# A decoder trunk in split fp32: high and low moving parts in one 512-wide product, value chunks in pairs

## The reference

```
for i in range(2):
    proj = x @ w_in[i]                                   # 1024 x 17408
    attn = three dilated window attentions, 8 heads of 128, merged by their log-sum-exp
    ret  = chunkwise retention, 4 heads, keys 256, values 512, group norm, * silu(gate)
    m    = (sig(x Wg_a) * (attn @ w_attn_proj) + sig(x Wg_r) * (ret @ w_ret_proj)) @ w_out
    x    = LayerNorm(alpha * x + m)
    ple  = sigmoid(x @ w_ple_gate) * (p[i] @ w_ple_proj)
    h    = causal_conv3(x @ w_up) + conv_b               # 2 * 2816 columns, per feature
    x    = LayerNorm(alpha * x + (gelu(gate) * up) @ w_down + ple)
```

## Time and profile before

| | us |
|---|---|
| median of 3 runs | 1545.26 (1545.22 to 1547.12) |
| the profiled execution | 1545.38 |
| its span | 1543.6 |
| TensorE busy | 1525.7 (99%), 11746 products |
| VectorE busy | 919.1 (60%) |
| ScalarE busy | 743.5 (48%) |
| DMA | 265.60 MB, mean 172 GB/s |

### The profile page before, as it was taken

How to read it: one execution, slowest core, us unless ns; L and a number is a source line. 1 busy time by engine, 2 the same in 40 slices (tenths; PEclk the granted TensorE clock), 3 DMA queues, 4 the chain that set the end, 5 groups by cost and what they waited for, 6 DMA issues and landing times.

```text
span 1543.6 us, 27813 instructions
## 1 busy us (share of the span) xinstructions
PE 1525.7 (99%) x11746; PEld 1478.3 (96%) x11746; DVE 919.1 (60%) x1001; ACT 743.5 (48%) x783; POOL 22.9 (1%) x23
## 2 busy tenths in 40 slices
PE   8999999999999999999999999999999999999998
PEld 7999999999999989999999999999999999899997
DVE  5564653745644486666865636556465445776677
ACT  5444454444533345556544534545445333465553
POOL 0000000000000010000000000000000000100000
PEclk9999999999999999999999999999999999999999
DMA  8544544445446565656455544454454464655551
GB/s 287 185 146 155 177 151 163 136 163 163 164 152 205 177 207 176 205 176 218 164 164 164 164 153 163 136 176 148 150 181 145 165 218 151 218 191 188 179 196 63
DMA packets 231462, 265.60 MB, mean 172 GB/s; under 512 B 4192, under 2 KB 221792, under 8 KB 230880
## 3 DMA queue, kind: packets, MB, share of 16 engines
q1 hardware_dynamic: 231248, 264.44, 51.8%
q10 hardware_dynamic: 144, 0.13, 0.0%
HBM read 263.50 MB, written 1.05 MB: 171 GB/s over the span
## 4 chain that ended last, share of the span: by engine, by line
PE 93%; DVE 4%; DMA 1%; ACT 1%; issue 1%; SPq 0%; DVEq 0%
PE bank L1029 26%; PE bank L1030 26%; PE bank L1031 26%; PE acc L1029 3%; PE acc L1030 3%; PE acc L1031 3%; DVE w_lo L605 1%; PE acc L1126 1%; PE acc L1144 1%; PE acc L1111 1%; PE acc L1141 1%; PE acc L1128 1%; DVE stat L627 1%; DMA raw<-w_in 1%; ACT w_hi L360 0%
## 5 line engine op out<-in xcount | busy, mean ns | idle before, releaser
L605 DVE TENSOR_TENSOR w_lo<-raw,w_hi 128x2048 fp32r<-128x2048 f32 x241 | 551.6, 2291 | 449.7 <-ACT w_hi L360 449.4
L1029 PE MATMUL bank<-xT_hi,w_hi 128*128 128x256 f32 x2240 | 637.0, 284 | 0.1
L1031 PE MATMUL bank<-xT_hi,w_lo 128*128 128x256 f32 x2240 | 633.8, 283 | 0.0
L1030 PE MATMUL bank<-xT_lo,w_hi 128*128 128x256 f32 x2240 | 633.8, 283 | 0.0
L360 ACT ACTIVATE w_hi<-raw 128x2048 fp32r<-128x2048 f32 x243 | 463.8, 1910 | 158.0 <-PE bank L1031 98.6
L1029 PEld LDWEIGHTS bank<-xT_hi,w_hi 128*128 128x128 f32 x2240 | 429.8, 192 | 2.0 <-issue 0.5
L1030 PEld LDWEIGHTS bank<-xT_lo,w_hi 128*128 128x128 f32 x2240 | 429.8, 192 | 1.5
L1031 PEld LDWEIGHTS bank<-xT_hi,w_lo 128*128 128x128 f32 x2240 | 429.8, 192 | 0.0
L1029 PE MATMUL bank<-w_hi,xT_hi 128*128 128x256 f32 x768 | 219.7, 286 | 5.4 <-DVE w_lo L605 2.3
L1030 PE MATMUL bank<-w_lo,xT_hi 128*128 128x256 f32 x768 | 217.2, 283 | 0.0
L1031 PE MATMUL bank<-w_hi,xT_lo 128*128 128x256 f32 x768 | 217.2, 283 | 0.0
(11 more groups left out here) (155 smaller groups left out, 1445.2 us busy)
## 6 DMA issues: line engine op xcount, KB each, us to landing
raw<-w_in SPq DMA_DIRECT2D x135, 1024.0 KB, 5.0
raw<-w_up SPq DMA_DIRECT2D x44, 1024.0 KB, 5.1
raw<-w_down SPq DMA_DIRECT2D x20, 1024.0 KB, 5.2
raw<-w_ret_proj SPq DMA_DIRECT2D x16, 1024.0 KB, 5.2
raw<-w_attn_proj SPq DMA_DIRECT2D x8, 1024.0 KB, 5.1
raw<-w_out SPq DMA_DIRECT2D x8, 1024.0 KB, 5.1
raw<-w_ple_gate SPq DMA_DIRECT2D x8, 1024.0 KB, 5.1
scratch<-ln_rows SPq DMA_DIRECT2D x4, 1024.0 KB, 7.0
```

The source lines that it names most:

```text
L605: nc.vector.tensor_tensor(w_lo[:, s, :], raw[:, s, :], w_hi[:, s, :].bitcast(F32), ALU.subtract).then_inc(lo_ready, 1)
L1029: mm(dst, st_hi, mv_hi, start=start, stop=False)
L1030: mm(dst, st_hi, mv_lo, start=False, stop=False)
L1031: return mm(dst, st_lo, mv_hi, start=False, stop=stop)
```

## The change

- **Merge and MLP (`both_parts`).** High and low parts of the moving operands (`xT_both`, `attn`, `ret`) now lie side by side. The high weights are multiplied with both in one 512-wide product: columns 0 to 255 hold high x high, 256 to 511 high x low. The product low x high, 256 wide, is added to the right part. A chunk fills two banks (a `pair`). ScalarE copies the right part out, VectorE adds the left part from PSUM to it, and what follows (sigmoid, centre tap) reads the sum. The very last up chunk of a layer stays in three narrow products (`one_part`).
- **Value chunks in pairs (`two_chunks`).** Two neighbouring slots of the weight ring are the moving operand of one 512-wide product, for retention values and for values of groups 1 and 2; one token half fills one bank. Both chunks must be ready at the start, both are freed at the end. Since a pair must not wrap round the ring, the order of a mixer differs between the layers (`VALUES`). The first pair of layer 0 stays as it was.
- **Written out.** The loops over mixers and merges become Python loops on all engines; the MLP keeps its loop.
- **Orders.** In a mixer the second `scores` stands behind chunk 13, VectorE's second mask and the group statistics stand at chunk 14 ahead of `to_lo`. In the first merge attention stands behind the first retention chunk. In the MLP `to_hi` and `to_lo` of the next chunk stand between take and centre or taps.

The core of the diff:

```diff
+VALUES = ((0, 2, 12, (11, 14)), (1, 0, 11, (13, 14)))   # rv, v0, v12, g01 of each layer
...
+            def both_parts(l, g, c, p, src, k0=0, first=True, last=True):
+                weights_ready(g, c)
+                hi, lo = w_hi[:, slot(l, c), :], w_lo[:, slot(l, c), :]
+                for m in range(2):
+                    for k in range(KT):
+                        o = k * CH + m * P
+                        mm(pair[p][:, m, :], hi[:, o:o + P], src[:, k0 + k, :, :].rearrange("p a t -> p (a t)"),
+                           start=first and k == 0, stop=False)
+                        ins = mm(pair[p][:, m, SEQ:2 * SEQ], lo[:, o:o + P], src[:, k0 + k, 0, :],
+                                 start=False, stop=last and k == KT - 1)
+                ins.then_inc(chunk_done, 1)
...
+            def two_chunks(l, c, b, t, ks=range(KT)):
+                s = slot(l, c)
+                for k in ks:
+                    ins = split_product(bank[b][:, :].rearrange("p (u n) -> p u n", u=2),
+                                        xT_hi[:, k, t * P:(t + 1) * P], xT_lo[:, k, t * P:(t + 1) * P],
+                                        w_hi[:, s:s + 2, k * CH:(k + 1) * CH], w_lo[:, s:s + 2, k * CH:(k + 1) * CH],
+                                        k == 0, k == KT - 1)
+                if t:
+                    ins.then_inc(chunk_done, 2)
+                elif ks[-1] == KT - 1:
+                    ins.then_inc(tile_done, 1)
...
     # ScalarE, MLP
+                def take_low(g, c, half, n):
+                    act.wait_ge(chunk_done, g + c + 1 + RING)
+                    act.wait_ge(mid_ready, n)
+                    nc.scalar.activation(hpad[:, 2 * half:2 * half + 2, 2:2 + SEQ], pair[half][:, :, SEQ:2 * SEQ],
+                                         ACT.Copy).then_inc(up_low, 1)
+                def take_centre(half, i):
+                    act.wait_ge(bank_read[2 * half], value(i + (l * USES[2 * half] + U_MLP[2 * half] + 2)))
+                    centre(hpad[:, 2 * half:2 * half + 2, 2:2 + SEQ], half, i).then_inc(up_centre, 1)
...
                 def steady(g, r, i):
                     to_hi(l, g, r, 3)
                     to_hi(l, g, r, 4)
                     mid_high(n)
-                    take_h(g, 2, 0, n, i + 1)
+                    take_low(g, 2, 0, n)
                     to_hi(l, g, r, 5)
+                    take_centre(0, value(i + 1))
                     gelu(value(l * NF + i + 1))
-                    take_h(g, 3, 1, n, i + 1)
+                    take_low(g, 3, 1, n)
+                    take_centre(1, value(i + 1))
...
     # VectorE, MLP
+                def up_sum(half, i):
+                    dve.wait_ge(up_low, value(2 * i + (l * (2 * NF - 1) + half + 1)))
+                    v = hpad[:, 2 * half:2 * half + 2, 2:2 + SEQ]
+                    nc.vector.tensor_tensor(v, pair[half][:, :, 0:SEQ], v, ALU.add).then_inc(bank_read[2 * half], 1)
...
                 def steady(g, i):
                     to_lo(l, g, 3)
                     to_lo(l, g, 4)
-                    gated(turn, value(nm + i + 1))
-                    taps(0, next_turn, i + 1)
+                    gated(value(l * NF + i), value(nm + i + 1))
+                    up_sum(0, value(i + 1))
                     to_lo(l, g, 5)
-                    taps(1, next_turn, i + 1)
+                    taps(0, value(i + 1))
+                    up_sum(1, value(i + 1))
+                    taps(1, value(i + 1))
...
     # TensorE, first merge
-                gate(g, 1, 1, 0)
-                attend((l + 1) * NJ)
-                pe.wait_ge(ret_affine, (l + 1) * NJ + 1)
-                pe.wait_ge(ret_lo_ready, (l + 1) * NJ)
-                mixers(g, 2, 0)
+                gate(g + 1, 1, 0)
+                pe.wait_ge(ret_affine, (l + 1) * NJ + 1)
+                transpose_prob((l + 1) * 2 * NJ)
+                pe.wait_ge(ret_lo_ready, (l + 1) * NJ)
+                pair_free(0, U_MERGE[0] + 1)
+                both_parts(l, L0, g + 2, 0, ret, 0, last=False)
+                attend((l + 1) * NJ)
+                both_parts(l, L0, g + 3, 0, ret, KT, first=False)
```

More of the change, by code:

```diff
@@ L183, in program @@
         half_neg = stat[:, 60:62]
-        bank = [ctx.enter_context(nc.psum_tensor(f"bank{i}", [P, 512], F32)) for i in range(4)]
+        pair = [ctx.enter_context(nc.psum_tensor(f"bank{i}", [P, 2, 512], F32)) for i in range(2)]
+        bank = [pair[i // 2][:, i % 2, :] for i in range(4)]
         acc = [ctx.enter_context(nc.psum_tensor(f"acc{i}", [P, 512], F32)) for i in range(4)]
-        ret_yT = (bank[3], acc[3])
         raw_loaded = [sem(f"raw_loaded{s}") for s in range(RING)]
@@ L726, in mixer @@
             def mixer(l, j):
-                it = value(l * NJ + j)
-                it2 = value(it * 2)
-                g = value(l * C_LAYER + j * C_MIX)
-                first = isinstance(j, int)
+                it = l * NJ + j
+                it2 = it * 2
+                g = l * C_LAYER + j * C_MIX
+                rv, v0, v12, g01 = VALUES[l]
+                one_by_one = l == 0 and j == 0
                 def rotate(i):
@@ new lines, in group_stats @@
+                def group_stats():
+                    dve.wait_ge(ret_av_done, it + 1)
+                    for t, av in enumerate((bank[3], acc[3])):
+                        ins = nc.vector.bn_stats(st_gn[:, t * 6:(t + 1) * 6], av[:, :])
+                    ins.then_inc(gn_stats, 1)
+                    dve.wait_ge(gn_stats, it + 1)
+                    nc.vector.memset(stat[:, 75:76], 0.0)
+                    for t in range(TT):
+                        ins = nc.vector.bn_aggr(mv_gn[:, t, :], st_gn[:, t * 6:(t + 1) * 6])
+                    ins.then_inc(gn_mean_var, 1)
+                    dve.wait_ge(gn_mean_var, it + 1)
+                    nc.vector.tensor_scalar(ve_gn, mv_gn[:, :, 1], GN_EPS, None, ALU.add).then_inc(gn_var_eps, 1)
@@ L804, in mixer @@
+                    if not l and j and c == 1:
+                        finish_ret(j - 1, it)
                     if c == 9:
@@ L910, in taps @@
                             ins.then_inc(conv_first, 1)
[L911 removed]
+                            dve.wait_ge(conv_first, value(2 * turn + (half + 1)))
                     ins.then_inc(conv_ready, 1)
@@ L1010, in _ @@
                 group_rstd(l, 0)
-                with pool.Fori(1, NJ) as j:
+                for j in range(1, NJ):
                     group_rstd(l, j)
@@ L1132, in mixer, with bank_free @@
             def mixer(l, j):
-                it = value(l * NJ + j)
-                it2 = value(it * 2)
-                g = value(l * C_LAYER + j * C_MIX)
-                used = [value(l * USES[b] + j * 5) for b in range(3)]
-                first = isinstance(j, int)
+                it = l * NJ + j
+                it2 = it * 2
+                g = l * C_LAYER + j * C_MIX
+                used = [l * USES[b] + j * 5 for b in range(3)]
+                rv, v0, v12, g01 = VALUES[l]
+                def bank_free(c):
+                    pe.wait_ge(bank_read[c % 3], used[c % 3] + c // 3 + 1)
                 def scores(a):
@@ L1216, in mixer @@
                         ins.then_inc(ret_av_done, 1)
+                begin = 0 if j else 3
+                if not j and not l:
+                    bank_free(0)
+                    x_tile_ready(0, 0)
+                    pe.wait_ge(first_lo, 1)
+                    token_half(l, 0, 0, 0, range(4))
+                    pe.wait_ge(x_in[1], 16)
+                    for h in range(2):
+                        transpose_half(0, 1, h)
+                    weights_ready(g, 0)
+                    token_half(l, 0, 0, 0, range(4, KT))
+                    x_tile_ready(0, 1)
+                    token_half(l, 0, 0, 1)
+                    for c in (1, 2):
+                        bank_free(c)
+                        by_token(l, g, c, c)
+                if not j and l:
+                    x_tile_ready(2 * l, 0)
+                    bank_free(0)
+                    weights_ready(g, 0)
+                    token_half(l, 0, 0, 0)
+                    bank_free(1)
+                    weights_ready(g, 2)
+                    two_chunks(l, 1, 1, 0, range(4))
+                    transpose_x(2 * l - 1, 1)
+                    two_chunks(l, 1, 1, 0, range(4, KT))
+                    x_tile_ready(2 * l, 1)
+                    token_half(l, 0, 0, 1)
+                    bank_free(2)
+                    two_chunks(l, 1, 2, 1)
+                for c in range(begin, C_MIX):
+                    if c in (rv + 1, v12 + 1):
+                        behind(c)
+                        continue
+                    bank_free(c)
+                    if c in (rv, v12):
+                        weights_ready(g, c + 1)
+                        two_chunks(l, c, c % 3, 0)
+                        bank_free(c + 1)
+                        two_chunks(l, c, (c + 1) % 3, 1)
+                    elif c == v0:
+                        by_token(l, g, c, c % 3)
```

(4 more changed lines are left out.)

549 lines of the change are left out of this document (312 added, 237 removed).

## The result

| | before | after |
|---|---|---|
| median of the runs shown | 1545.24 us (1545.13 to 1547.12) | 1578.25 us (1576.58 to 1580.46) |
| profiled execution, its span | 1545.38, 1543.6 | 1578.85, 1577.0 |
| mean granted clock | 0.999 | 0.993 |

What follows compares the result with a forecast made beforehand. TensorE, 99% busy with matmuls, was taken to bound the kernel. Terms -8.4 - 9.6 + 27.8 + 5.0 + 5.3 + 0.2 + 3 = +23.3 us on 1545.4 gave 1569; range 1552 to 1582, own mechanism 1558 to 1576.

Steps and rivals of the forecast that it cites:

- The ring: MLP loop: ScalarE and VectorE's chain of waits sets a period of 17.25 us against 16.98; TensorE waits 0.7 per iteration.
- Rival 1: MLP: the ring doesn't bind and TensorE sets the pace throughout, 1529 us; chance 0.11, and 0.04 for a half-way case.
- The tail: Written-out MLP end: TensorE waits 4.6, 0.6, 2.6 and 5.0 us; the whole MLP stage +13.9 a layer.
- Products: Merge and MLP chunks: a wide and narrow pair takes 346.5 ns, 0.21 us saved per chunk, 8.4 us outside the MLP.
- the prediction's own sign: TensorE: the prediction is wrong if the MLP shows no waits or wide steps differ from 226.5 ns.
- Value pairs: Mixers: a pair of value chunks takes 48 x 226.5 ns, 0.64 us less; 15 pairs save 9.6 us.
- layer 1's mixers: Layer 1: pairs find their weights 3 us early; mixers about 1.3 us shorter each, -5.1 for the stage.
- Between gated mixture and MLP: From the gated mixture's start to the first MLP chunk: forecast 0 change.
- Mixers of layer 0: Value pairs wait 1.8 us for their second weight chunk, three times, +5.3 us; the stage +0.8.
- Merges' waits: New copies and sums cost +1.35 us at the last merge and +1.1 at the first, a layer; together +5.0.
- Clock: Behind the MLP's last long wait: six to twelve products at half clock, 1.5 us a layer, +3.
- rival 3: MLP tails: cold clock spreads, each of four long waits costs 3 us, bare; 1578 us, chance 0.12.

Runs made afterwards that it cites:

- e1: Changed kernel, in the MLP loop alone ScalarE forms the centre tap before copying the next weights and VectorE runs taps before splitting them; 1566.2 us, ratio 1.0136.
- e4: Changed kernel with the MLP's wide and narrow up chunks as 48 products of 256 columns again, takes, sums and order kept; 1578.14 us, ratio 1.0213.
- e3: Changed kernel with a tile's eight wide products first and its eight narrow ones after, instead of by turns; 1575.03 us, ratio 1.02.
- e7: Changed kernel with e2, e3 and e5 together, bank 3 awaited only before the second up half, last weights' copy and split one turn earlier; 1545.53 us.
- e5: Changed kernel, in layer 0's mixers VectorE splits the value pair's second weight chunk ahead of mask and group statistics; 1571.84 us, ratio 1.0166.
- e2: As e1, and in the written-out MLP tail too the centre and taps come before the next weights' copy and split; 1558.47 us, ratio 1.0083.
- e6: Changed kernel with useless wide products (17 and 18) filling TensorE's two long waits in each MLP tail; 1575.01 us, ratio 1.0187.
- e8: As e7, with the tail's next to last w_down chunk copied and split one place earlier; 1550.64 us, ratio 1.0029.
- e9: As e8, with VectorE's residual and last-weight split cut into halves between sums and taps, and ScalarE's last-weight copy ahead of its rounding; 1540.22 us, ratio 0.9962.
- e11: As e9, with ScalarE's take of the whole last up half ahead of GELU in each MLP tail; 1531.78 us, ratio 0.991.
- e10: As e9, with 15 useless wide products in TensorE's wait for each layer's last intermediate; 1536.74 us, ratio 0.9942.

## Why the prediction was right, and where it was off

- **The ring.** Right: 17.30 us measured for 17.25, take to taps 4.62 for 4.71. TensorE's wait in each turn is 0.3 in the rows where 0.7 was foretold, since its own turn is 16.8 and not 16.5. e1 takes the order away and the loss with it, e4 takes the products away and nothing happens. Rival 1 (the ring doesn't bind) is out.
- **The tail.** Right in kind and nearly in size: waits of 4.3 and 4.7 us for 4.6 and 5.0; the stage +14.65 for +13.9. The 2.6 us for weights foretold between them came as 0.64 (layer 0) and 1.59 (layer 1).
- **Products.** The mis-sized term. The prediction put a pair at 226.5 + 120 = 346.5 ns everywhere; by turns it takes 353.4 in the merges and nearly everywhere in the MLP, and only a few MLP chunks have 347. By the prediction's own sign (wide steps that differ from 226.5) this part failed: by turns a wide step is 230 to 240 ns. In the merges, of a layer's 4.2 us, 2.1 arrived: 4.3 us of the miss. In the MLP it was hidden in after; it makes TensorE's turn 16.79 instead of 16.5 in e1. e3 shows half of it to be the order of the two widths (350 in groups); why the other 3.5 ns stay, and why a few chunks are quicker, no run tells. Value pairs step at 227 ns as taken, and layer 1's mixers gave 4.7 of 5.1.
- **Between gated mixture and MLP.** Missed: the written-out entry waits for banks 1 and 3 ahead of the first half, and bank 3 is read last. 1.0 us a layer; e7 removed it. The step "a change adds a wait, who is queued behind it" wasn't made for this one.
- **Mixers of layer 0.** Three waits of 1.95, 1.63 and 1.63 us where 1.8 each were foretold, gone in e5. The stage is 1.7 over its forecast all the same. 0.8 of that is the kernel's start. In after TensorE's first products on weights step by 213 ns until 14.4 us, in before by 120 (after above, before below, the two rows three products apart):

```profile
12.00 0.41 PE L1179 MATMUL bank<-w_hi,xT_both 128*128 128x256 f32 x1
...
12.64 0.41 PE L1179 MATMUL bank<-w_hi,xT_both 128*128 128x256 f32 x1
```

```profile
11.73 0.28 PE L1029 MATMUL bank<-w_hi,xT_hi 128*128 128x256 f32 x1
...
12.09 0.28 PE L1029 MATMUL bank<-w_hi,xT_hi 128*128 128x256 f32 x1
```

  At one and the same product of the first mixer, some 62 us in, after is 0.8 us behind before, e4 0.75 ahead, e2 and e6 1.45 behind. From there to the first merge the stage is 1.7 us longer than before in after, e3, e4 and e6 alike, so 0.9 over the forecast. 0.6 of the 0.9 is the price of the waits: without them e5 passes this stretch 5.9 us faster, where 5.3 was put down. In e1 and e2 the stretch is 3.3 us longer than before: there the clock stood at its lower level for 3.4 us behind the first of the three waits. The 213 ns are 256 columns at 1.2 GHz, so the start was slow by the clock, it seems; the profile's record of the clock begins only at 14.4 us in after, and doesn't show it.
- **Merges' waits.** 1.35 on the last, as worked out; 0.9 us of 1.1 at the first retention chunk.
- **Clock.** +3 forecast; in e6 the last products were 4.3 us shorter in sum and the MLP 1.5 longer, and the median fell by 3.2. The Trainium skill (TensorE: Matmul & The Clock Gate, "Why this matters for your kernels") advises against idle gaps between bursts; the waits of 4.3 and 4.7 us, followed by 6.7 us at half clock each in layer 0 and by 3.4 in layer 1, agree.
- **A number shared with a rival.** The result is the very figure of rival 3 (1578), but not by its mechanism. That rival had each of the four long waits cost 3 us by the clock, 12 in all; e6 fills all four and gets 3.2 back. The difference to 1569 is made of the terms below.

Of the 33.5 us between the profiled executions the forecast had 23.3. The other 10.2: 4.3 from the pair's step, 2.0 from bank 3, 1.5 from the MLP, 2.1 from the mixers (0.8 of it the start), 0.3 behind it.

My later expectations were worse than the forecast. e2, e7 and e8 each took a wait's length for its price. In a tail of rings a wait that goes uncovers the next: from e7 on, where TensorE and the last intermediate came within 0.7 and 1.6 us of each other, only what brought both earlier (e9, e11) or kept the clock up (e10) made the kernel faster.

## What to carry to other kernels

A saving of 13 ns per folded product (in value pairs; 7 where widths go by turns) was real, but it was worth nothing until the order in which the two helper engines do their passes was redone: count the ring (who takes, who is queued between take and the next step) before the matmuls. Put long passes that nobody waits for into the places where the engine is idle within the chain, cut to the length of that idle time (here 2.2 us cut in two for slots of 1.16; the place and the cut were tried together only). Before moving a late split, follow the chain to the last product; and if a wait must be long, place it where cold products behind it are covered.

## What the runs showed of the hardware

- Products of different width by turns cost more than in groups: 353 ns for a 512 and a 256 by turns in the merges and most of the MLP, 350 in groups (e3); in a few MLP chunks 347 by turns.
- The granted clock fell to half in waits of 3.8 (e9) and 4.3 to 4.7 us (after), and at the end of one of 2.4 (e6), not in one of 1.65 (e11). It stayed there for 3.4 us in e6, e9 and layer 1 of after and for 6.7 in layer 0 of after, though TensorE had products again within 2 us in each. Length alone doesn't decide it: a wait of 1.94 us at the first value pair was followed by 3.4 us at half clock in e1 and e2, and by none in after, e3, e4 and e6.
- A kernel's start varies: the first 256-wide products on weights stepped by 120 ns in the profiled executions of before, e9 and e11 and by 213 ns in those of after and e6, and by 62 us the traces lie up to 2.6 us apart.
- The same wait costs by its place: with cover behind it, e7 ran its last products in 11.55 us; with it moved to the last intermediate, e8 took 14.23.
